# Residual norms by column halves, with a weight subtraction and a cast moved to GpSimd

## The chip, the cores and the metric

One NeuronCore of a Trainium2 chip runs the whole program. The metric is device time in microseconds of that core; each kernel is executed several times and the median stands for it. TensorE is the matrix engine; VectorE (DVE in the profile), ScalarE (ACT) and GpSimd (POOL) do elementwise work; SyncE (SP) issues the DMA transfers. PSUM is the memory of eight banks of 512 fp32 columns that TensorE writes into.

## The reference

The program computes four transformer layers on 256 tokens of width 1024, in fp32: an RWKV-7 layer and an MLA layer with a convolutional gated feed-forward (2816 hidden features) each, then two layers with other attentions and a squared-ReLU MLP. The change is about the first two:

```python
def rmsnorm(x, g):
    xf = x.astype(jnp.float32)
    y = xf * lax.rsqrt(jnp.mean(xf * xf, axis=-1, keepdims=True) + NORM_EPS)
    return (y * g.astype(jnp.float32)).astype(x.dtype)
...
        x = x + rmsnorm(m, norm_g[layer, 1])
        f = conv_ffn(rmsnorm(x, norm_g[layer, 2]), ffn_w_in[layer], ffn_conv_w[layer],
                     ffn_conv_b[layer], ffn_w_out[layer])
        x = x + rmsnorm(f, norm_g[layer, 3])
```

Here m is the output of the layer's mixer behind its output projection, and the norm of a product stands ahead of each addition to x.

## The kernel before, in words

**Data.** The 256 tokens are two tiles (t = 0, 1) of 128 partitions; `x` and `xn` hold 2 x 1024 columns. A product of width 1024 for tile t stands in PSUM banks 2t (columns 0 to 511) and 2t + 1 (columns 512 to 1023). fp32 accuracy comes from splitting each operand into a rounded part (`Ah`, `Bh`, `hTh`, `hidh`) and the rest (`Al`, `Bl`, `hTl`, `hidl`), and adding three products. The rounded weights are made by ScalarE (`round_slot` L1775, `round_a` L1785, `round_b` L1794), the rests by VectorE (`rest_slot` L2514, `rest_a` L2521, `rest_b` L2528) and, for a few slots, by GpSimd (`rest_slot`, L2303).

**Order.** Each engine runs its own program in order; semaphores tie them together. Nothing is planned at run time: the order of each queue is written out by hand.

**Output projection** (`out_proj`, `split_slot`, L877): the first weight slot fills banks 0 and 2, the second banks 1 and 3. The products of tile 0 and then of tile 1 each raise `m_rdy`. Behind it TensorE runs filler products on constants (`keep`, L837) and then `turn16`, which transposes x for the next matmuls. In front of the feed-forward layers this is a product with a diagonal matrix that holds the reciprocal root of the norm (`xn_rdy`, L802), tile by tile; behind them it is a plain transposition that waits for x alone (L800).

**Sites 1 and 3: the norm behind the output projection.** ScalarE (`res_root`, L1745, L1746) squares 1024 columns with a sum and takes the root; VectorE (`res_norm`, L2449, L2450, L2454) takes the reciprocal, scales by it and by the gain row, and adds to x. ScalarE (`norm`, L1699, L1700) squares the new x and takes the root, and VectorE (L2423, L2424) builds the diagonal. On ScalarE `ffn_start(.., 0)`, the cast of the first feed-forward weights, stands ahead of `res_root`, and on VectorE its subtraction stands ahead of `res_norm`.

**The feed-forward** (`ffn`) walks over 11 chunks of 256 hidden features in two halves. `first` (L963 to L971) makes the hidden features, `second` (L991) multiplies them by the second weights into banks 0 to 3, six products per tile and half. The last chunk ends with `second(ch, 0)` and `second(.., 1, last_one=True)`: all of tile 0, then all of tile 1.

**Sites 2 and 4: the norm behind the feed-forward.** VectorE (`res_late`, L2462) multiplies 1024 columns by the gain, ScalarE (`res_root`, L1742) squares the raw product in PSUM behind it and takes the root, and VectorE (L2466, L2468) adds the scaled product to x. Of one PSUM bank, only one of the two engines reads at a time. Behind site 2 ScalarE casts the query weights (`round_m(1)`, L2023, `qdh`), then casts the turned x for the MLA layer (`h2h`, L2084), takes its norm (`late_norm`, L1707, L1714) and casts `hTh` (L2091); VectorE makes the rests (L2917, L3025, L2506) and the latent norm (L2992, L2998), for which TensorE waits (L1339).

Of the kernel before, what the change touches and what calls it, by code (L numbers as in the profile page):

```python
# [84 lines left out]
def program(nc, d, out_d):  # L85
# [4 lines left out]
    with ctx:  # L90
# [30 lines left out]
        gt = sb("gt", [P, 4 * 64])  # L121

# [34 lines left out]
        class Carve:  # L157
# [4 lines left out]
            def __call__(self, n):  # L162
# [16 lines left out]
        a_used = sem("a_used")  # L179
        ah_rdy = sem("ah_rdy")  # L180
# [69 lines left out]
              ["hi", "lo",  # L250
# [527 lines left out]
        def _(pe):  # L778
# [5 lines left out]
            def turn16(name):  # L784
# [143 lines left out]
            def ffn(w, nf):  # L928
# [47 lines left out]

                def second(ch, half, first_one=False, last_one=False):
# [30 lines left out]
                def step(ch, par):  # L1008
# [5 lines left out]
                    second(ch, 0)  # L1014

                chunk_walk(pe, w, step)
                second(NCH[w] - 1, 1, last_one=True)
# [325 lines left out]
            def down(i, b0, w, hi, lo, hi_rdy, lo_rdy):  # L1343
# [4 lines left out]
                pe.wait_ge(dn["hi"], i + 1)  # L1348
# [126 lines left out]
            pe.wait_ge(dn["hi"], 4)  # L1475
# [7 lines left out]
            for s in range(2):  # L1483
                pe.wait_ge(dn["hi"], 5 + s)
# [177 lines left out]
        def _(act):  # L1662
# [74 lines left out]
            def res_root(mi):  # L1737
                for t in range(NT):
                    m = ps[:, 2 * t:2 * t + 2, :].rearrange("p b n -> p (b n)")
                    if mi in MG:  # L1740
                        act.wait_ge(mg_rdy, 2 * MG[mi] + t + 1)
                        link(A_(m, m, ACT.Square, accum_out=st[:, 8 + t:9 + t]))  # L1742
                    else:
                        act.wait_ge(m_rdy, 2 * mi + t + 1)
                        link(A_(xn[:, t, :], m, ACT.Square, accum_out=st[:, 8 + t:9 + t]))  # L1745
                    A_(st[:, 10 + t:11 + t], st[:, 8 + t:9 + t], ACT.Sqrt, bias=eps, scale=1.0 / D  # L1746
                       ).then_inc(msd_rdy, 1)
# [279 lines left out]
            res_root(1)  # L2027
            round_m(1, a_loaded[a_qd], 32 * (a_at["qd"] // 2 + 1))
# [120 lines left out]
            for half in range(2):  # L2149
                round_slot(a_at["wo1"] + 1, half)  # L2150
            ffn_start("ffn1", 0)
            res_root(2)
            norm("nf1")
# [4 lines left out]
            res_root(3)  # L2158
# [108 lines left out]
        def _(pool):  # L2267
# [29 lines left out]

            def rest_slot(a, half):
# [101 lines left out]
        def _(dve):  # L2400
# [43 lines left out]
            def res_norm(mi, gain, following):  # L2444

                dve.wait_ge(rows_in, 16)
                for t in range(NT):
                    dve.wait_ge(msd_rdy, 2 * mi + t + 1)
                    link(V.reciprocal(st[:, 12 + t:13 + t], st[:, 10 + t:11 + t]))  # L2449
                    link(V.scalar_tensor_tensor(xn[:, t, :], mview(t), st[:, 12 + t:13 + t], row(gain),  # L2450
                                                ALU.mult, ALU.mult))
                    if t == 1:
                        norm(following, [0])
                    V.tensor_tensor(x[:, t, :], x[:, t, :], xn[:, t, :], ALU.add).then_inc(x_done, 2)  # L2454
                dve.wait_ge(x_done, x_at(mi, 1))

            def res_late(mi, gain):

                dve.wait_ge(rows_in, 16)
                for t in range(NT):  # L2460
                    dve.wait_ge(m_rdy, 2 * mi + t + 1)
                    V.tensor_tensor(xn[:, t, :], mview(t), row(gain), ALU.mult).then_inc(mg_rdy, 1)  # L2462
                dve.wait_ge(mg_rdy, 2 * MG[mi] + 2)
                for t in range(NT):
                    dve.wait_ge(msd_rdy, 2 * mi + t + 1)
                    link(V.reciprocal(st[:, 12 + t:13 + t], st[:, 10 + t:11 + t]))  # L2466
                    for o0, o1 in ((0, D),) if t == 0 else ((0, 512), (512, D)):
                        V.scalar_tensor_tensor(x[:, t, o0:o1], xn[:, t, o0:o1], st[:, 12 + t:13 + t],  # L2468
                                               x[:, t, o0:o1], ALU.mult, ALU.add
                                               ).then_inc(x_done, (o1 - o0) // 512)  # L2470
                dve.wait_ge(x_done, x_at(mi, 1))

            def res_plain(mi, name=None):
                if name:
                    late_scale(name)
                for t in range(NT):
                    if t == 0 or not name:
                        dve.wait_ge(m_rdy, 2 * mi + t + 1)
                    for o0, o1 in ((0, D),) if t == 0 else ((0, 512), (512, D)):
                        if t and name:  # L2480
                            if o0:
                                dve.wait_ge(m_rdy, 2 * mi + 2)
                            else:
                                dve.wait_ge(half_rdy, {"nm0": 1, "nm1": 2}[name])
# [422 lines left out]
            ffn_start("ffn0", 0)  # L2907
            res_norm(0, "g0_res", "nf0")
            norm("nf0", [1])
            turned_split("nf0", "g0_ffn")  # L2910
            ffn_start("ffn0", 1)
            ffn("ffn0", 0)

            def rest_m(i):

                dve.wait_ge(dn["hi"], i + 1)
# [453 lines left out]
```

## Time and profile before

| | us |
|---|---|
| median of 3 runs | 1356.43 |
| lowest and highest | 1354.27, 1356.81 |
| the profiled execution | 1354.54 |
| its span, first to last instruction | 1352.8 |
| TensorE busy | 1318.0 (97%) |
| VectorE busy | 934.7 (69%) |
| ScalarE busy | 654.6 (48%) |
| GpSimd busy | 96.2 (7%) |

Busy times are sums over the whole span; an engine that is not the last to finish in a stage may stand still at no cost. The chain that ended last is followed back from the last instruction, at each step to what released it. Times within the span count from its first instruction.

### The profile page before, as it was taken

Reading aid. Unit: us, or ns where it says so; the run is one execution under the profiler, and the core shown is the slowest. Engines: PE = TensorE matmul, PEld = TensorE weight load, DVE = VectorE, ACT = ScalarE, POOL = GpSimd, SP = SyncE. Lnnn points to the kernel's source line nnn. Section 1 sums busy time; section 2 is a strip of 40 time slices with the busy share of each in tenths; the row PEclk is TensorE's granted clock in tenths of the full one; section 3 lists DMA queues with packets and bytes.
Section 4 is the critical chain, followed back from the end, with each engine's and each line's share of the span. In section 5 each row is a group of like instructions: output and inputs, shape, how many; then the busy total and the mean of one; then the engine's idle time right before and its main releaser. Section 6 shows DMA issues by size and latency. Waiting matters only on the chain.

```text
span 1352.8 us, 23308 instructions
## 1 busy us (share of the span) xinstructions
PE 1318.0 (97%) x9276; PEld 1134.2 (84%) x9276; DVE 934.7 (69%) x1613; ACT 654.6 (48%) x977; POOL 96.2 (7%) x97
## 2 busy tenths in 40 slices
PE   7999999999999999999999998999999999999999
PEld 5987987888888988888888887888888888888887
DVE  6783356877777775877777588666666796576664
ACT  4431323644445775644444577543334568444441
POOL 0003153000000020000001000000001042000000
PEclk9999999999999999999999999999999999999999
DMA  8531213655553233665551550874531432573610
GB/s 241 215 125 64 66 65 99 226 190 192 192 163 110 70 125 112 219 196 189 186 186 62 187 187 1 311 296 171 202 125 63 165 113 75 205 285 138 243 62 32
DMA packets 111126, 208.10 MB, mean 154 GB/s; under 512 B 3872, under 2 KB 53408, under 8 KB 110528
## 3 DMA queue, kind: packets, MB, share of 16 engines
q1 hardware_dynamic: 111040, 206.88, 44.6%
q8 instruction: 62, 1.02, 0.3%
q14 instruction: 24, 0.20, 0.0%
HBM read 205.82 MB, written 1.05 MB: 153 GB/s over the span
## 4 chain that ended last, share of the span: by engine, by line
PE 85%; DVE 8%; ACT 5%; issue 1%; POOL 0%; DMA 0%; SPq 0%; DVEq 0%; ACTq 0%; POOLq 0%
PE ps L991 21%; PE ps L966 18%; PE ps L877 11%; PE ps L971 10%; PE ps L1060 2%; PE ps L1029 2%; PE ps L1377 2%; PE ps L1163 2%; PE ps L1284 1%; PE ps L942 1%; DVE Al L2514 1%; ACT Ah L1775 1%; PE ps L1420 1%; PE ps L1434 1%; ACT arena L2060 1%
## 5 line engine op out<-in xcount | busy, mean ns | idle before, releaser
L966 PE MATMUL ps<-hTx,Ah 128*128 128x512 f32 x1088 | 270.7, 391 | 0.0
L2521 DVE TENSOR_TENSOR Al<-ringA,Ah 128x2048 fp32r<-128x2048 f32 x76 | 173.8, 2287 | 103.4 <-ACT Ah L1785 103.4
L966 PEld LDWEIGHTS ps<-hTx,Ah 128*128 128x128 f32 x1088 | 199.8, 188 | 38.4
L971 PEld LDWEIGHTS ps<-hTx,Al 128*128 128x128 f32 x1152 | 156.7, 191 | 10.6
L971 PE MATMUL ps<-hTx,Al 128*128 128x256 f32 x1152 | 160.7, 283 | 0.0
L1820 ACT COPY xn<-ps 128x512 f32<-128x512 f32 x72 | 42.3, 587 | 243.6 <-PE ps L971 236.3
L1785 ACT CAST Ah<-ringA 128x2048 fp32r<-128x2048 f32 x76 | 145.8, 1919 | 16.7 <-PE ps L877 13.9
L1794 ACT CAST Bh<-ringB 128x1024 fp32r<-128x1024 f32 (+1 forms) x76 | 107.1, 1409 | 89.5 <-PE ps L991 89.5
L877 PE MATMUL ps<-Ah,hTx 128*128 128x512 f32 (+1 forms) x576 | 136.2, 387 | 1.1 <-ACT hTx L1765 0.9
L991 PE MATMUL ps<-Bh,hidh 128*128 128x512 f32 x432 | 135.0, 392 | 1.6 <-issue 1.1
L991 PE MATMUL ps<-Bl,hidh 128*128 128x512 f32 x432 | 134.3, 390 | 0.0
L2528 DVE TENSOR_TENSOR Bl<-ringB,Bh 128x1024 fp32r<-128x1024 f32 (+1 forms) x76 | 126.9, 1670 | 10.5 <-ACT Bh L1794 10.0
L991 PE MATMUL ps<-Bh,hidl 128*128 128x512 f32 x432 | 134.0, 390 | 0.0
L877 PEld LDWEIGHTS ps<-Ah,hTx 128*128 128x128 f32 x576 | 106.3, 188 | 23.2 <-issue 2.5
L2514 DVE TENSOR_TENSOR Al<-ringA,Ah 128x2048 fp32r<-128x2048 f32 x30 | 68.6, 2289 | 42.4 <-ACT Ah L1775 42.3
L991 PEld LDWEIGHTS ps<-Bl,hidh 128*128 128x128 f32 x432 | 81.1, 188 | 17.6
L991 PEld LDWEIGHTS ps<-Bh,hidl 128*128 128x128 f32 x432 | 81.2, 188 | 17.4
L1775 ACT CAST Ah<-ringA 128x2048 fp32r<-128x2048 f32 (+1 forms) x38 | 71.4, 1878 | 38.5 <-PE ps L877 35.0
L991 PEld LDWEIGHTS ps<-Bh,hidh 128*128 128x128 f32 x432 | 76.4, 189 | 13.8 <-issue 2.3
L2548 DVE TENSOR_TENSOR xn<-ps,xn 128x512 f32<-128x512 f32 x68 | 46.8, 688 | 51.9 <-ACT xn L1820 51.9
L877 PE MATMUL ps<-Al,hTx 128*128 128x512 f32 (+1 forms) x288 | 70.8, 386 | 0.3 <-POOL Al L2303 0.3
L877 PEld LDWEIGHTS ps<-Al,hTx 128*128 128x128 f32 x288 | 53.5, 188 | 11.3 <-POOL Al L2303 0.7
(433 smaller groups left out, 2013.4 us busy)
## 6 DMA issues: line engine op xcount, KB each, us to landing
ringA<-in_ffn_w_in SPq DMA_DIRECT2D x44, 1024.0 KB, 7.5
ringA<-in_mlp_w SPq DMA_DIRECT2D x32, 1024.0 KB, 7.5
ringB<-in_mlp_w SPq DMA_DIRECT2D x32, 1024.0 KB, 6.9
ringB<-in_ffn_w_out SPq DMA_DIRECT2D x44, 512.0 KB, 4.3
ringA<-in_diff_w_in SPq DMA_DIRECT2D x12, 1024.0 KB, 6.3
ringA<-in_dsa_w_in SPq DMA_DIRECT2D x8, 1024.0 KB, 6.4
ringA<-in_w_k SPq DMA_DIRECT2D x4, 1024.0 KB, 8.3
ringA<-in_w_r SPq DMA_DIRECT2D x4, 1024.0 KB, 7.2
```

The lines of the kernel that those rows point to most:

```text
L877: ins = mm(ps[:, banks[t], 0:n], left[:, k, t * P:(t + 1) * P], right[:, half, (k % 4) * n:(k % 4) * n + n], start=(start and k == 0), sto ...
L966: mm(o.rearrange("p (i t) -> p i t", i=2), w_hi, hTx[:, :, k * T:(k + 1) * T], start=(k == 0), stop=False)
L971: last = mm(o[:, T:2 * T], Al[:, half, k * T + j * P:k * T + j * P + P], hTh[:, k, :], start=False, stop=(k == KT - 1))
L991: last = mm(ps[:, 2 * t + c_, :], hb[:, half, f * T + t * P:f * T + t * P + P], wb[:, half, o:o + 512], start=(first_one and f == 0 and i ...
L1775: nc.scalar.copy(k_half(Ah[:, half, :], a, 0), k_half(ringA[:, a % 2, :], a, half)).then_inc(ah_rdy, 1)
L1785: nc.scalar.copy(a_split(w, Ah, half), a_half(w, ap, half)).then_inc(ah_rdy, 1)
L1794: nc.scalar.copy(Bh[:, half, 0:n], ringB[:, bp, half * n:(half + 1) * n]).then_inc(bh_rdy, 1)
L1820: nc.scalar.copy(gup if gelu else hsum, ps[:, b:b + 2, c0:c0 + T]).then_inc(lo_rdy, 1)
L2514: V.tensor_tensor(k_half(Al[:, half, :], a, 0), k_half(ringA[:, a % 2, :], a, half), k_half(Ah[:, half, :], a, 0).bitcast(F32), ALU.subtra ...
L2521: V.tensor_tensor(a_split(w, Al, half), a_half(w, (a_at[w] + par) % 2, half), a_split(w, Ah, half).bitcast(F32), ALU.subtract).then_inc(al ...
L2528: V.tensor_tensor(Bl[:, half, 0:n], ringB[:, (G0[w] + par) % 2, half * n:(half + 1) * n], Bh[:, half, 0:n].bitcast(F32), ALU.subtract).the ...
L2548: V.tensor_tensor(out, ps[:, b:b + 2, T:2 * T], out, ALU.add).then_inc(hs_rdy, 1)
```

## The change

It works on column halves, which are also PSUM banks.

1. In `res_norm` (sites 1 and 3) VectorE multiplies the product by the gain first, half by half; those of columns 0 to 511 of both tiles are done while the second weight slot is still being multiplied. ScalarE squares each half by itself, turns the sum of the first half into a part mean (sum / 1024 + eps, an Identity operation on one column) and takes the root of the second half's sum / 1024 plus that. VectorE then does x + xn * factor in one operation per half. The sums of the new x are formed likewise.
2. The same for `res_late` (sites 2 and 4), in another order, with ScalarE squaring the second bank first into another bank.
3. The last 24 products of the gated feed-forwards are reordered in `second_pair`: tile 0 is whole after 15 products, the first bank of tile 1 after 18.
4. The subtraction of `ffn_start(.., 0)` goes from VectorE to GpSimd (`rest_first`); on ScalarE the first halves' squares stand ahead of its cast.
5. The cast of the query weights goes from ScalarE, ahead of `h2h`, to GpSimd (`dn["hq"]`).
6. Of the two filler products between the turns at sites 1 and 3 one remains.

```diff
@@ PE, turn16
-                                    keep(2, 0)
+                                    keep(1, 0)
@@ PE
+                def second_pair(ch):
+
+                    parts = ((hidh, Bh), (hidh, Bl), (hidl, Bh))
+
+                    def product(half, t, c_):
+                        for i in range(3):
+                            hb, wb = parts[i]
+                            ins = mm(ps[:, 2 * t + c_, :], hb[:, half, t * P:t * P + P],
+                                     wb[:, half, c_ * 512:c_ * 512 + 512],
+                                     start=False, stop=(half == 1 and i == 2))
+                        return ins
+
+                    pe.wait_ge(bl_rdy, ch * 2 + (2 * g0 + 1))
+                    pe.wait_ge(h_rdy, ch * 2 + (2 * g0 + 1))
+                    product(0, 0, 0)
+                    product(0, 0, 1)
+                    product(0, 1, 0)
+                    pe.wait_ge(bl_rdy, ch * 2 + (2 * g0 + 2))
+                    pe.wait_ge(h_rdy, ch * 2 + (2 * g0 + 2))
+                    product(1, 0, 0)
+                    product(1, 0, 1).then_inc(m_rdy, 1)
+                    product(1, 1, 0).then_inc(half_rdy, 1)
+                    product(0, 1, 1).then_inc(b_used, 1)
+                    product(1, 1, 1).then_inc(m_rdy, 1)
...
-                    second(ch, 0)
+                    if nf == 1 and isinstance(ch, int) and ch == NCH[w] - 1:
+                        second_pair(ch)
+                    else:
+                        second(ch, 0)
@@ ScalarE
-            def res_root(mi):
...
+            def square(dst, src, at, ready=None):
+
+                ins = A_(dst, src, ACT.Square, accum_out=hs[:, at:at + 1])
+                if ready is None:
+                    link(ins)
+                else:
+                    ins.then_inc(sq_rdy, 1)
+                    act.wait_ge(sq_rdy, ready)
+
+            def part_mean(dst, at):
+
+                link(A_(hs[:, dst:dst + 1], hs[:, at:at + 1], ACT.Identity, bias=eps, scale=1.0 / D))
+
+            def whole_root(dst, at, part):
+
+                return A_(st[:, dst:dst + 1], hs[:, at:at + 1], ACT.Sqrt, bias=hs[:, part:part + 1],
+                          scale=1.0 / D)
+
+            def res_late_root(mi):
+
+                for t, first, out in ((0, 1, 4), (1, 3, 0)):
+                    act.wait_ge(m_rdy, 2 * mi + t + 1)
+                    square(ps[:, out, :], ps[:, first, :], 4 * t, ready=2 * mi + t + 1)
+                    part_mean(4 * t + 1, 4 * t)
+                    act.wait_ge(wm_rdy, 2 * mi + t + 1)
+                    square(ps[:, first - 1, :], ps[:, first - 1, :], 4 * t + 2)
+                    whole_root(10 + t, 4 * t + 2, 4 * t + 1).then_inc(msd_rdy, 1)
+
+            def first_halves(mi):
+
+                for t in range(NT):
+                    act.wait_ge(wm_rdy, 2 * mi + t + 1)
+                    square(ps[:, 2 * t, :], ps[:, 2 * t, :], 4 * t)
+                    part_mean(4 * t + 1, 4 * t)
+
+            def res_norm(mi):
+
+                def own(t):
+                    act.wait_ge(m_rdy, 2 * mi + t + 1)
+                    square(ps[:, 2 * t, :], ps[:, 2 * t + 1, :], 4 * t + 2, ready=2 * mi + t + 1)
+                    whole_root(10 + t, 4 * t + 2, 4 * t + 1).then_inc(msd_rdy, 1)
+
+                def summed(t, half):
+                    o = slice(512 * half, 512 * half + 512)
+                    act.wait_ge(x_done, x_at(mi, t, half))
+                    square(xn[:, t, o], x[:, t, o], 8 + 4 * t + 2 * half)
+                    if half:
+                        whole_root(2 + t, 10 + 4 * t, 9 + 4 * t).then_inc(rms_rdy, 1)
+                    else:
+                        part_mean(9 + 4 * t, 8 + 4 * t)
+
+                own(0)
+                summed(0, 0)
+                own(1)
+                summed(0, 1)
+                summed(1, 0)
+                summed(1, 1)
@@ ScalarE's order, layer 0 (layer 1 likewise, without the query weights)
+            first_halves(0)
             ffn_start("ffn0", 0)
-            res_root(0)
-            norm("nf0")
+            res_norm(0)
...
-            res_root(1)
-            round_m(1, a_loaded[a_qd], 32 * (a_at["qd"] // 2 + 1))
+            res_late_root(1)
@@ GpSimd
+            def rest_first(w):
+
+                pool.wait_ge(al_rdy, S0[w])
+                pool.wait_ge(ah_rdy, S0[w] + 1)
+                G.tensor_tensor(a_split(w, Al, 0), a_half(w, a_at[w] % 2, 0),
+                                a_split(w, Ah, 0).bitcast(F32), ALU.subtract).then_inc(al_rdy, 1)
...
+            rest_first("ffn0")
+            pool.wait_ge(a_loaded[a_qd], 32 * (a_at["qd"] // 2 + 1))
+            pool.wait_ge(dn["hi"], 1)
+            G.tensor_copy(MW[1][0], MW[1][1]).then_inc(dn["hq"], 1)
             for half in range(2):
                 rest_slot(a_at["wo1"], half)
+            rest_first("ffn1")
@@ VectorE, res_norm
-                for t in range(NT):
-                    dve.wait_ge(msd_rdy, 2 * mi + t + 1)
-                    link(V.reciprocal(st[:, 12 + t:13 + t], st[:, 10 + t:11 + t]))
-                    link(V.scalar_tensor_tensor(xn[:, t, :], mview(t), st[:, 12 + t:13 + t], row(gain),
-                                                ALU.mult, ALU.mult))
-                    if t == 1:
-                        norm(following, [0])
-                    V.tensor_tensor(x[:, t, :], x[:, t, :], xn[:, t, :], ALU.add).then_inc(x_done, 2)
+                dve.wait_ge(*a_free[2 * SPLIT[a_at["wo%d" % (mi // 2)]] + 1])
+                for t in range(NT):
+                    weighted(t, lo).then_inc(wm_rdy, 1)
+                dve.wait_ge(sq_rdy, 2 * mi + 1)
+                link(weighted(0, hi))
+                root(0)
+                summed(0, lo)
+                summed(0, hi)
+                dve.wait_ge(sq_rdy, 2 * mi + 2)
+                link(weighted(1, hi))
+                root(1)
+                summed(1, lo)
+                norm(following, [0])
+                summed(1, hi)
@@ VectorE, res_late
+                dve.wait_ge(m_rdy, 2 * mi + 1)
+                weighted(0, lo).then_inc(wm_rdy, 1)
+                dve.wait_ge(sq_rdy, 2 * mi + 1)
+                weighted(0, hi)
+                dve.wait_ge(half_rdy, mi // 2 + 1)
+                weighted(1, lo).then_inc(wm_rdy, 1)
+                root(0)
+                summed(0, lo)
+                dve.wait_ge(sq_rdy, 2 * mi + 2)
+                link(weighted(1, hi))
+                summed(0, hi)
+                root(1)
+                summed(1, lo)
+                summed(1, hi)
@@ VectorE's order
-            ffn_start("ffn0", 0)
             res_norm(0, "g0_res", "nf0")
             norm("nf0", [1])
             turned_split("nf0", "g0_ffn")
+            dve.wait_ge(al_rdy, S0["ffn0"] + 1)
             ffn_start("ffn0", 1)
```

`weighted(t, o)` is a product of the PSUM columns with the gain row into `xn`, `summed(t, o)` is x + xn * reciprocal root in one operation, and `root(t)` the reciprocal. Waits on `dn["hi"]`, `half_rdy` are renumbered.

## Rows read from the trace of the kernel before

**Rows 1.** The page: TensorE's granted clock by slices, the chain's shares by engine.
```profile
PEclk9999999999999999999999999999999999999999
...
PE 85%; DVE 8%; ACT 5%; issue 1%; POOL 0%; DMA 0%; SPq 0%; DVEq 0%; ACTq 0%; POOLq 0%
```

**Rows 2.** Timeline, site 1: start, length, engine, line, operation, tiles, shapes, count.
```profile
229.63 2.29 DVE L2514 TENSOR_TENSOR Al<-ringA,Ah 128x2048 fp32r<-128x2048 f32 x1 [3.15 <-ACT Ah L1775]
...
233.07 1.91 ACT L1785 CAST Ah<-ringA 128x2048 fp32r<-128x2048 f32 x1 [3.48 <-PE ps L877]
...
235.79 1.03 ACT L1745 ACTIVATE xn<-ps 128x1024 f32<-128x1024 f32 x1 [0.81 <-PE ps L877]
...
236.94 0.29 ACT L1746 ACTIVATE st<-st,con 128x1 f32<-128x1 f32 x1
...
238.32 3.19 PE L837 MATMUL ps<-con 128*128 128x256 f32 x14
...
242.30 2.05 PE L802 MATMUL ps<-arena,x 128*128 128x128 f32 x16 [0.80 <-DVE arena L2424]
...
245.53 2.05 PE L802 MATMUL ps<-arena,x 128*128 128x128 f32 x16 [0.31 <-DVE arena L2424]
```

**Rows 3.** Timeline, site 3: the turn of tile 1.
```profile
548.55 2.05 PE L802 MATMUL ps<-arena,x 128*128 128x128 f32 x16 [0.31 <-DVE arena L2424]
```

**Rows 4.** Timeline, site 2.
```profile
426.67 2.11 ACT L2023 CAST kvdh<-ringA 128x2304 fp32r<-128x2304 f32 x1
...
430.27 2.52 DVE L2462 TENSOR_TENSOR xn<-ps,rows 128x1024 f32<-128x1024 f32 x2 [2.44 <-PE ps L991]
...
434.24 2.77 ACT L2023 CAST qdh<-ringA 128x3072 fp32r<-128x3072 f32 x1
...
434.68 2.18 PE L800 MATMUL ps<-con,x 128*128 128x128 f32 x16 [0.56 <-DVE x L2468]
434.74 1.42 DVE L2468 SCALAR_TENSOR_TENSOR x<-xn,st,x 128x512 f32<-128x512 f32 x2
...
436.90 3.02 ACT L2084 ACTIVATE h2h<-ps,cols 128x256 fp32r<-128x256 f32 x8
```

**Rows 5.** The chain that ended last, behind site 2: start, length, what.
```profile
443.15 3.23 DVE hTx L2506 x8
```

**Rows 6.** Timeline, site 4.
```profile
732.32 0.70 PE L991 MATMUL ps<-Bh,hidh 128*128 128x512 f32 x2 [0.51 <-DVE hidl L2619]
...
738.44 2.18 PE L800 MATMUL ps<-con,x 128*128 128x128 f32 x16 [0.55 <-DVE x L2468]
...
739.79 3.03 ACT L1765 ACTIVATE hTx<-ps,cols 128x256 fp32r<-128x256 f32 x8 [1.70 <-PE ps L800]
```

**Rows 7.** The page's groups: count, busy us, mean ns of one, idle before.
```profile
L1820 ACT COPY xn<-ps 128x512 f32<-128x512 f32 x72 | 42.3, 587 | 243.6 <-PE ps L971 236.3
...
L2548 DVE TENSOR_TENSOR xn<-ps,xn 128x512 f32<-128x512 f32 x68 | 46.8, 688 | 51.9 <-ACT xn L1820 51.9
```

**Rows 8.** GpSimd's subtractions and copy, and VectorE beside them (groups, then timeline).
```profile
L2303 POOL TENSOR_TENSOR Al<-ringA,Ah 128x2048 fp32r<-128x2048 f32 x6 | 27.4, 4564 | 342.7 <-ACT Ah L1775 297.6 <-DVE arena L3239 45.0
...
L2316 POOL COPY rows<-con 128x512 f32<-128x512 f32 x1 | 0.6, 609 | 5.8 <-DMA con<-in_con 5.8
...
1106.90 3.04 POOL L2303 TENSOR_TENSOR Al<-ringA,Ah 128x1312 fp32r<-128x1312 f32 x1 [3.12 <-ACT Ah L1775]
...
1106.96 3.12 DVE L3010 TENSOR_TENSOR arena<-arena 128x128 f32<-128x128 f32 x1
1110.01 0.28 DVE L3011 TENSOR_TENSOR arena<-arena 128x128 f32<-128x128 f32 x1
```

**Rows 9.** Timeline, TensorE's first records.
```profile
4.99 2.93 PE L832 MATMUL ps<-con 128*128 128x128 f32 x12 [4.99 <-DMA con<-in_con]
...
9.80 1.50 PE L832 MATMUL ps<-con 128*128 128x128 f32 x12
```

**Rows 10.** Timeline, ScalarE, between the last Gelu and the first Sqrt of site 2.
```profile
425.26 1.28 ACT L1688 ACT_TABLE_LOAD   x1
```

More of the change, by code:

```diff
@@ L121, in program @@
         gt = sb("gt", [P, 4 * 64])
+        hs = sb("hs", [P, 16])
         Ah = over("Ah", "arena", 0, [P, 2, 2048])
@@ L179, in program @@
         a_used = sem("a_used")
+        wm_rdy, sq_rdy = sem("wm_rdy"), sem("sq_rdy")
         ah_rdy = sem("ah_rdy")
@@ L249, in program @@
         dn = {n: sem("dn_" + n) for n in
-              ["hi", "lo",
+              ["hi", "hq", "lo",
                "h2", "l2",
@@ L1013, in step @@
                     first(ch, 1, single=isinstance(ch, int) and ch == NCH[w] - 1)
-                    second(ch, 0)
+                    if nf == 1 and isinstance(ch, int) and ch == NCH[w] - 1:
+                        second_pair(ch)
+                    else:
+                        second(ch, 0)
                 chunk_walk(pe, w, step)
-                second(NCH[w] - 1, 1, last_one=True)
+                if nf == 2:
+                    second(NCH[w] - 1, 1, last_one=True)
             def feature_job(a0, j0, s, xi):
@@ L2150, in _ @@
                 round_slot(a_at["wo1"] + 1, half)
+            first_halves(2)
             ffn_start("ffn1", 0)
-            res_root(2)
-            norm("nf1")
+            res_norm(2)
             turned_split("nf1", "g1_ffn")
@@ L2157, in _ @@
             prime(ACT.Sqrt)
-            res_root(3)
+            res_late_root(3)
             turned_split("n2", "n0_mix")
@@ L2444, in res_norm, with weighted, root, summed @@
             def res_norm(mi, gain, following):
-                dve.wait_ge(rows_in, 16)
-                for t in range(NT):
+                lo, hi = slice(0, 512), slice(512, D)
+                def weighted(t, o):
+                    return V.tensor_tensor(xn[:, t, o], mview(t)[:, o], row(gain)[:, o], ALU.mult)
+                def root(t):
                     dve.wait_ge(msd_rdy, 2 * mi + t + 1)
                     link(V.reciprocal(st[:, 12 + t:13 + t], st[:, 10 + t:11 + t]))
-                    link(V.scalar_tensor_tensor(xn[:, t, :], mview(t), st[:, 12 + t:13 + t], row(gain),
-                                                ALU.mult, ALU.mult))
-                    if t == 1:
-                        norm(following, [0])
-                    V.tensor_tensor(x[:, t, :], x[:, t, :], xn[:, t, :], ALU.add).then_inc(x_done, 2)
+                def summed(t, o):
+                    V.scalar_tensor_tensor(x[:, t, o], xn[:, t, o], st[:, 12 + t:13 + t], x[:, t, o],
+                                           ALU.mult, ALU.add).then_inc(x_done, 1)
@@ L2455, in res_norm @@
+                summed(1, lo)
+                norm(following, [0])
+                summed(1, hi)
                 dve.wait_ge(x_done, x_at(mi, 1))
             def res_late(mi, gain):
[L2459 to L2464, printed above, removed]
+                lo, hi = slice(0, 512), slice(512, D)
@@ L2465, in res_late, with weighted, root, summed @@
+                def weighted(t, o):
+                    return V.tensor_tensor(xn[:, t, o], mview(t)[:, o], row(gain)[:, o], ALU.mult)
+                def root(t):
                     dve.wait_ge(msd_rdy, 2 * mi + t + 1)
                     link(V.reciprocal(st[:, 12 + t:13 + t], st[:, 10 + t:11 + t]))
[L2467 to L2470, printed above, removed]
+                def summed(t, o):
+                    V.scalar_tensor_tensor(x[:, t, o], xn[:, t, o], st[:, 12 + t:13 + t], x[:, t, o],
+                                           ALU.mult, ALU.add).then_inc(x_done, 1)
@@ L2914, in rest_m @@
             def rest_m(i):
-                dve.wait_ge(dn["hi"], i + 1)
+                dve.wait_ge(*((dn["hi"], 1), (dn["hq"], 1), *((dn["hi"], j) for j in (2, 3, 4, 5)))[i])
                 V.tensor_tensor(MW[i][2], MW[i][1], MW[i][0].bitcast(F32), ALU.subtract
@@ L3086, in _ @@
             turned_split("nf1", "g1_ffn")
+            dve.wait_ge(al_rdy, S0["ffn1"] + 1)
             ffn_start("ffn1", 1)
```

19 lines of the change are left out of this document (6 added, 13 removed).

## The prediction

> **What bounds the kernel now.** I read the page first. TensorE carries 85% of the chain that ended last [rows 1], so nearly everything else is hidden, and a change off TensorE can pay only where TensorE stands still. The change touches four such places, the residual norms behind the two output projections (sites 1 and 3) and behind the two gated feed-forward layers (sites 2 and 4). I then read the timeline of each. At site 1 the projection gives way to filler at 238.32, which lasts until 241.51, and the turn of tile 1 starts only at 245.53 [rows 2]. Between them lies a strict alternation: ScalarE squares 1024 columns, VectorE scales, adds, ScalarE squares the new x, roots, VectorE builds the diagonal. Site 3 is the same to a few hundredths, 303.02 us later [rows 3]. At site 2 what ends last is not the norm: the turns of tile 1 can be read from about 436.0, but ScalarE is in the cast of `qdh` (2.77 us) and starts `h2h` at 436.90; the chain of waits then runs through `h2h` to `hTl` [rows 4, 5]. Site 4 is a norm followed by turns at 738.44 [rows 6].
>
> **Prices.** ScalarE's square of 1024 PSUM columns holds the chain 1.15 us (235.79 to 236.94) [rows 2]; I take the same from SBUF, with 0.03 more. A ScalarE copy of 512 columns lasts 0.587 against 1.03 for 1024, 0.44 less [rows 2, 7]; so I take 0.72 and 0.75 for a square of 512. One-column roots take 0.30 [rows 2]; Identity on one column is not in the trace, and the root is its nearest row: 0.30. VectorE from PSUM, 512 columns: 0.69 [rows 7]; the in-place sum in SBUF, 512: 0.71, half of 1.42 [rows 4].
>
> **Sites 1 and 3, queue by queue.** VectorE ends the last `rest_slot` at 231.92 [rows 2], weights the two first halves until 233.3 (hidden). ScalarE squares them and forms the part means: 2 x (0.72 + 0.30) = 2.05, from 232.65 to 234.7. But behind them in its queue stands the cast for the feed-forward, which before ran at 233.07; it now ends at 236.65 (1.91), and `own(0)`, whose data are ready at 235.79, starts 0.88 late. Then: square 0.72, weighting of the second half 0.69 with the root beside it, reciprocal and its waits 0.25, so the first sum could start at 238.4. With order `own(0), summed(0,0), own(1), ...` the rest is sum 0.71, square 0.75, mean 0.30, square 0.72, weighting 0.69, reciprocal 0.25, sums 0.71, diagonal, sum 0.71, square 0.75, root 0.30, diagonal 0.55: with hand-overs of 0.03 to 0.10 the turn of tile 1 comes at 245.7, against 245.53: +0.2. One filler product is dropped (`keep(1, 0)`), about 0.5 us; it fits a tile-0 turn now at 243.3 instead of 242.30. So without contention the halves give nothing: what is saved on the four squares of 1024 columns (4.7 us) goes to six late ones of 512 (4.4), two means between them (0.6) and the late cast.
>
> The moved subtraction is what decides. On VectorE such a one is 2.29 us, behind the cast and hidden: `res_root` had its data only at 235.79 [rows 2]. On GpSimd it takes about 4.56 us [rows 8], needs the cast, and so runs from 236.7 to 241.2. Its result is needed at 247.3, so by itself it is hidden. But it overlaps the first sum, which reads two SBUF tensors (`xn` and `x`). What that does is in the trace: L3010, 128 columns from two SBUF tensors, lasts 3.12 us from 1106.96, while its twin L3011 right behind takes 0.28; GpSimd's subtraction ran from 1106.90 to 1109.94. So VectorE's instruction was held until about 0.15 us before the end of GpSimd's row. The "GPSIMD Engine Reference" of the Trainium skill (section "Specifications") lists exactly this, contention of the shared SBUF interface with VectorE instructions that have two SBUF inputs; the trace agrees, with 3.12 against 0.28. VectorE reading one PSUM and one SBUF tensor is not held (512-column PSUM rows keep 0.69), so the weightings pass. The first sum is held from 238.4 to 241.05, 2.65 us, and as `own(1)` is queued behind `summed(0,0)`, everything after it slides with it. Site 1: +0.2 + 2.65 = +2.85; with the same at site 3, **+5.7**. Bounds per site: +0.2 if nothing is held, +3.2 if held to the very end of a 4.63 us instruction and the late cast costs a little more.
>
> **Site 2.** `second_pair` reorders 24 products, at 0.23 each the same sum. Tile 0 is whole after 15 products instead of 18: 0.69 earlier, 429.58 instead of 430.27 [rows 4]. From there VectorE: weightings 3 x 0.69, reciprocal 0.2, sum 0.71, weighting 0.69, sum 0.71 = 4.5 us to the end of tile 0, so the turn starts near 434.15 instead of 434.68. The `qdh` cast leaves ScalarE for GpSimd: `h2h` starts when the first pair of banks is turned. At site 4 that is 1.35 after the first turn [rows 6], here 435.5 instead of 436.90: -1.4. VectorE must follow: `rest_m(0)` and `h2l` end at 441.5, just before `hTl` may start at 441.65 instead of 443.15, so the gain passes on down the chain [rows 5]. GpSimd's cast of 3072 columns starts at 428.8, when `kvdh` is cast [rows 4], if the query weights are loaded by then; by its one copy row, 0.609 for 512 [rows 8], it lasts at most 6 x 0.609 = 3.65 and ends by 432.5, 0.5 past the first sum at 431.9; part of that hold is in slack. I take **-1.3**; bounds -1.5, and by GpSimd's two-input rate (4.56/2048 x 3072 = 6.8 us, held until 435.5) +2.3. Its own consumer, `rest_m(1)`, comes at 445, nine microseconds later.
>
> **Site 4.** Here the second half of the hidden features comes late: the products of the second half wait for VectorE's `hidl` until 732.32 [rows 6]. Before, 12 products stood ahead of that wait and 12 behind; now 9 and 15, so the last product ends 0.69 later, while tile 0 (6 products behind the wait) is no earlier. VectorE's 4.5 us from 733.99 give a turn at 738.6 against 738.44: **+0.15**, bounds 0 and +0.9.
>
> Sum: 5.7 - 1.3 + 0.15 = +4.55 us. The profiled execution took 1354.54 (span 1352.8), 1.9 below the median of 1356.43; on the median this gives **1361.0**. About 0.2%, 2.7 us, is what a measurement of this kernel can tell from no change.
>
> **The rivals.**
> *The hold does not occur* (chance 0.20): GpSimd and VectorE might share more finely where the operands lie otherwise. Then +0.4 - 1.3 + 0.15 = -0.75: 1355.7, no change to be told. Against it stands L3010 in rows 8, a single instruction, though ten times its length.
> *The clock falls as well* (0.25). In the hold TensorE stands still from 241.51 to about 246.0, 4.5 us, where before it paused 0.80 there [rows 2]. The only longer pause of the trace is the start, 4.99 us: the twelve records behind it take 2.93 us, the same twelve 1.50 us at 9.80 [rows 9], that is the lower of the two levels, 1.2 GHz, against 2.4; the page's PEclk line stays at 9 in both [rows 1], so durations alone show it. At 4.5 us the pause is nearer to 4.99 than to 0.8, but these are two points only. Price: 1.45 us per site, +4.55 + 1.45 = 1362.5 for one site, 1363.9 for both. The Trainium skill, "TensorE: Matmul & The Clock Gate" (section "Why this matters for your kernels"), says that idle gaps between bursts of matmuls put the clock back; by it this rival would be the forecast.
> *Faster* (0.08). Place: ScalarE's queue at 233 to 236.7. If the first halves come early enough to leave the cast at 233.07 and VectorE isn't held, `own(0)` starts on its data: -0.88 + 0.2 = -0.7 at each of sites 1 and 3, with -1.5 at site 2: -2.9, 1353.5. It needs the first halves done before 233.07; VectorE ends its subtraction only at 231.92, which leaves 1.15 for 2.05 of ScalarE work.
> *GpSimd's cast is slow* (0.03): 1364.6. *Identity needs another table than Sqrt* (0.02): a table load takes 1.28 us [rows 10], two for each of twelve means, 30.7 us, 1387. The Trainium skill, "ScalarE: Activation LUTs" (section "Table sets: the hidden batching unit"), says that identity is in every set; no row here shows it.
>
> **How the numbers follow.** The forecast has 0.42. The range, 1355.6 to 1363.6, reaches from no hold to a clock that falls at one site, and leaves out about 0.2. The forecast's own range is 1359 to 1362.5. Slower by over 0.2%: 0.42, less a tenth for an overestimated hold, plus 0.25 and 0.05, 0.68. Faster: 0.08. Within: the rest, 0.24.
>
> **What would show it.** At sites 1 and 3: GpSimd subtraction from 236.7 for 4.5 us; one sum of 512 columns of about 3.3 us instead of 0.7, ending with it; `own(0)` near 236.7; TensorE idle over 4 us. At site 2: no ScalarE cast between root and `h2h`, `h2h` near 435.5. At site 4: the last product 0.7 later. Wrong would be: sums of 0.7 us under the subtraction, a first half hidden well before 233, or records behind the pause at double length.

## The result, and the profile after

| | before | after |
|---|---|---|
| median of 5 runs, us | 1356.06 (1354.27 to 1356.81) | 1365.11 (1361.8 to 1365.29) |
| profiled execution, us | 1354.54 | 1363.4 |
| its span, us | 1352.8 | 1361.6 |
| its mean granted TensorE clock | 1.000 | 0.995 |

The ratio is 1.0064, with a 95% interval of 1.0053 to 1.0076: the changed kernel is slower by 8.7 us (9.05 between the medians), where +4.6 was forecast. It is slower, as forecast, but the time lies outside the range, whose upper end was 1363.6.

The page of the changed kernel, TensorE's clock by slices and the chain's shares. Before, every slice stood at 9 [rows 1]; now two slices of 34 us, those that hold sites 1 and 3, show 8.

```profile
PEclk9999999899999999899999999999999999999999
...
PE 86%; DVE 6%; ACT 6%; issue 1%; POOL 0%; DMA 0%; SPq 0%; ACTq 0%; DVEq 0%; POOLq 0%
```

The timeline of the changed kernel at site 1 (columns as in [rows 2]; the site comes 0.18 us later than before, by the end of the last projection product).

```profile
234.83 1.91 ACT L1862 CAST Ah<-ringA 128x2048 fp32r<-128x2048 f32 x1
...
236.64 0.58 ACT L1770 ACTIVATE ps<-ps 128x512 f32<-128x512 f32 x1
236.91 4.56 POOL L2378 TENSOR_TENSOR Al<-ringA,Ah 128x2048 fp32r<-128x2048 f32 x1 [20.82 <-ACT Ah L1862]
...
237.38 0.69 DVE L2537 TENSOR_TENSOR xn<-ps,rows 128x512 f32<-128x512 f32 x1 [4.07 <-ACT ps L1770]
...
238.30 4.38 DVE L2544 SCALAR_TENSOR_TENSOR x<-xn,st,x 128x512 f32<-128x512 f32 x2
...
242.05 0.63 ACT L1770 ACTIVATE xn<-x 128x512 f32<-128x512 f32 x1 [4.38 <-DVE x L2544]
...
245.98 3.79 PE L804 MATMUL ps<-arena,x 128*128 128x128 f32 x16 [4.29 <-DVE arena L2512]
...
249.56 1.06 PE L839 MATMUL ps<-con 128*128 128x256 f32 x2
250.41 2.16 PE L804 MATMUL ps<-arena,x 128*128 128x128 f32 x16
252.33 0.49 PE L944 MATMUL ps<-hTx,Ah 128*128 128x256 f32 x2
```

Two things are to be seen. The two sums at 238.30 take 4.38 us. The first of them alone takes 3.72 us, to 242.02, where one that nothing delays takes 0.75; GpSimd's subtraction ends at 241.47, so the sum was held until about 0.2 us before that end. I call this the hold. ScalarE's next square starts at 242.05. The second thing is on TensorE: the turn of tile 0 (its 16 transposing products) at 245.98, behind a pause of 4.29 us, takes 3.79 us where it took 2.05 [rows 2]. The windows show why (length, busy us of PE, PEld, DVE, ACT and POOL with counts, granted clock, DMA share, GB/s):

```profile
242.00:245.00 3.00, 0.00 (x0) 0.00 (x0) 1.76 (x5) 2.82 (x9) 0.00 (x0) 0.84 1.02 411
245.00:248.00 3.00, 2.02 (x9) 2.02 (x10) 1.71 (x5) 2.12 (x7) 0.00 (x0) 0.50 0.16 66
248.00:251.00 3.00, 3.00 (x15) 2.82 (x14) 0.29 (x1) 0.00 (x0) 0.00 (x0) 0.53 0.00 0
```

The granted clock is 0.50 there, the lower of the two levels (1.2 GHz). TensorE stood still until 245.98, and by shorter windows the clock falls near 244.0, in the pause, and comes back only near 250.8; the diagonal of tile 1 is ready at 248.3, but its turn waits for TensorE's own slow work until 250.41. At site 3 the same stretch reads:

```profile
543.23 4.55 POOL L2378 TENSOR_TENSOR Al<-ringA,Ah 128x2048 fp32r<-128x2048 f32 x1 [33.19 <-ACT Ah L1862]
...
544.65 4.34 DVE L2544 SCALAR_TENSOR_TENSOR x<-xn,st,x 128x512 f32<-128x512 f32 x2
...
552.29 3.78 PE L804 MATMUL ps<-arena,x 128*128 128x128 f32 x16 [4.30 <-DVE arena L2512]
...
556.72 2.58 PE L804 MATMUL ps<-arena,x 128*128 128x128 f32 x16
```

Sites 2 and 4 of the changed kernel, which answer to [rows 4, 6]:

```profile
431.70 2.11 ACT L2100 CAST kvdh<-ringA 128x2304 fp32r<-128x2304 f32 x1
...
433.94 2.76 POOL L2470 CAST qdh<-ringA 128x3072 fp32r<-128x3072 f32 x1 [192.47 <-ACT kvdh L2100]
...
436.85 0.75 DVE L2576 SCALAR_TENSOR_TENSOR x<-xn,st,x 128x512 f32<-128x512 f32 x1
...
440.39 3.03 ACT L2160 ACTIVATE h2h<-ps,cols 128x256 fp32r<-128x256 f32 x8 [1.73 <-PE ps L802]
...
740.91 0.47 PE L986 MATMUL ps<-Bh,hidh 128*128 128x512 f32 x1 [1.20 <-DVE hidl L2742]
...
748.41 3.04 ACT L1842 ACTIVATE hTx<-ps,cols 128x256 fp32r<-128x256 f32 x8 [1.73 <-PE ps L802]
```

From ScalarE's cast of `kvdh` to `h2h` it was 10.23 us and is 8.69: 1.54 gained. The gain is passed on: from the cast of `kvdh` to the start of the last projection product of site 3 it was 113.76 us and is 112.19. GpSimd's cast ends at 436.70, before the first sum, which keeps its 0.75 us. At site 4, from the product that waits for `hidl` to ScalarE's cast of the turned x, it was 7.47 and is 7.50.

**The account** (the other kernels are those of the next section). What runs before site 1 is the same in all of them, and yet the last projection product ends anywhere between 238.4 and 241.1 in their profiled executions. In the six where it ends last, at 239.2 or later, TensorE's granted clock is 0.91 in one stretch of 20 us (from 20 to 40 us, in `e2_filler` from 180 to 200), and in the other five it is 1.00 in every such stretch. So I measure each site by itself: from the end of the last projection product to the first feed-forward product (sites 1 and 3), and from `kvdh` to `h2h` (site 2). Each figure comes from the one execution that was profiled. Before, at site 1, that is from 237.41 + 1.08 to 247.34, which is 8.85:

```profile
237.41 1.08 PE L877 MATMUL ps<-Al,hTx 128*128 128x512 f32 x4
...
247.34 0.48 PE L942 MATMUL ps<-hTx,Ah 128*128 128x256 f32 x2
```

| kernel | site 1, us | site 3, us | site 2, us | sum of the three against before, us | ratio measured |
|---|---|---|---|---|---|
| before | 8.85 | 8.85 | 10.23 | | |
| after | 13.66 | 14.09 | 8.69 | +8.5 | 1.0064 [1.0053, 1.0076] |
| `e2_filler` | 11.50 | 11.52 | 8.69 | +3.8 | 1.0032 [1.0020, 1.0044] |
| `e3_sub_dve_cast_first` | 10.54 | 10.54 | 8.69 | +1.8 | 1.0009 [0.9999, 1.0018] |
| `e9_sub_dve_long_filler` | 9.07 | 9.07 | 8.69 | -1.1 | 0.9999 [0.9990, 1.0008] |
| `e8_split8` | 10.64 | 10.70 | 8.69 | +2.1 | 1.0012 [1.0003, 1.0021] |
| `e7_gpsimd_sub_only` | 9.54 | 9.49 | 10.23 | +1.3 | 1.0015 [1.0006, 1.0025] |
| `e10_short_filler` | 10.88 | 9.73 | 10.22 | +2.9 | 1.0026 [1.0014, 1.0038] |
| `e4_gpsimd_cast_only` | 8.85 | 8.85 | 9.36 | -0.9 | 0.9995 [0.9986, 1.0004] |
| `e5_late_no_gpsimd_cast` | 8.85 | 8.85 | 9.62 | -0.6 | 0.9996 [0.9987, 1.0005] |
| `e6_late_only` | 8.85 | 8.86 | 8.80 | -1.4 | 0.9989 [0.9980, 0.9998] |

A ratio of 0.001 is 1.36 us, and each sum lies within its measured interval. The loss sits at sites 1 and 3. The kernel before was timed again beside each group of experiments, with medians of 1355.50, 1355.04 and 1355.78 us, so the ratios are to be compared and not the bare medians.

### The profile page after: what moved, and what is told of

Same layout as the page of the kernel before. It is cut to its first block, busy times and chain, and to the rows that moved or that the text cites. A ratio compares the mean times of both kernels' runs of the same rounds, so it can differ in the third digit from the quotient of the medians.

```text
span 1361.6 us, 23361 instructions
## 1 busy us (share of the span) xinstructions
PE 1321.4 (97%) x9272; PEld 1137.9 (84%) x9272; DVE 937.8 (69%) x1625; ACT 658.8 (48%) x1012; POOL 108.1 (8%) x100
## 3 DMA queue, kind: packets, MB, share of 16 engines
HBM read 205.82 MB, written 1.05 MB: 152 GB/s over the span
## 4 chain that ended last, share of the span: by engine, by line
PE 86%; DVE 6%; ACT 6%; issue 1%; POOL 0%; DMA 0%; SPq 0%; ACTq 0%; DVEq 0%; POOLq 0%
PE ps L1018 21%; PE ps L968 18%; PE ps L879 11%; PE ps L973 10%; PE ps L1091 2%; PE ps L1060 2%; PE ps L1408 2%; PE ps L1194 2%; PE ps L1315 1%; PE ps L944 1%; ACT Ah L1852 1%; PE ps L804 1%; PE ps L1451 1%; PE ps L1465 1%; PE ps L839 1%
## 5 line engine op out<-in xcount | busy, mean ns | idle before, releaser
L2644 DVE TENSOR_TENSOR Al<-ringA,Ah 128x2048 fp32r<-128x2048 f32 x74 | 169.3, 2287 | 97.4 <-ACT Ah L1862 97.4
L1018 PE MATMUL ps<-Bh,hidh 128*128 128x512 f32 x416 | 129.9, 392 | 1.1 <-issue 1.1
L1018 PE MATMUL ps<-Bl,hidh 128*128 128x512 f32 x416 | 129.2, 390 | 0.0
L1018 PE MATMUL ps<-Bh,hidl 128*128 128x512 f32 x416 | 129.0, 390 | 0.0
L2637 DVE TENSOR_TENSOR Al<-ringA,Ah 128x2048 fp32r<-128x2048 f32 x30 | 68.6, 2289 | 42.4 <-ACT Ah L1852 42.2
L1018 PEld LDWEIGHTS ps<-Bl,hidh 128*128 128x128 f32 x416 | 78.1, 188 | 17.0
L1018 PEld LDWEIGHTS ps<-Bh,hidl 128*128 128x128 f32 x416 | 78.1, 188 | 16.7
L1018 PEld LDWEIGHTS ps<-Bh,hidh 128*128 128x128 f32 x416 | 73.6, 189 | 12.5 <-issue 1.4
```

What stands on the lines that cost most here:

```text
L1018: last = mm(ps[:, 2 * t + c_, :], hb[:, half, f * T + t * P:f * T + t * P + P], wb[:, half, o:o + 512], start=(first_one and f == 0 and i ...
L2637: V.tensor_tensor(k_half(Al[:, half, :], a, 0), k_half(ringA[:, a % 2, :], a, half), k_half(Ah[:, half, :], a, 0).bitcast(F32), ALU.subtra ...
L2644: V.tensor_tensor(a_split(w, Al, half), a_half(w, (a_at[w] + par) % 2, half), a_split(w, Ah, half).bitcast(F32), ALU.subtract).then_inc(al ...
```

## The experiments

**Is the lost time hold or clock?** The changed kernel with TensorE kept busy through the hold:

```diff
-            keep(7, 7)
+            keep(16, 7)
             turn16("nf0")
```
and the same for `nf1`.

> The changed kernel, with 16 filler products instead of 7 ahead of the turns at sites 1 and 3, so that TensorE does not stand still while VectorE is held. Nothing else differs. Theory (hold by GpSimd 2.7 us per site, and behind the 4.3 us pause some 2.1 us per site from TensorE at its lower level): the held sum stays at about 3.6 us, the turn of tile 0 takes 2.05 us again instead of 3.79, the turn of tile 1 starts about 2.7 us later than before instead of 4.7; in all about +4 us on before, near 1360. Rival (the slow turns come from the shorter filler between the turns, or from memory traffic, not from the pause): the turn stays near 3.8 us and the time near 1365.

```profile
240.70 4.38 DVE L2544 SCALAR_TENSOR_TENSOR x<-xn,st,x 128x512 f32<-128x512 f32 x2
240.91 7.07 PE L839 MATMUL ps<-con 128*128 128x256 f32 x32
...
248.38 2.05 PE L804 MATMUL ps<-arena,x 128*128 128x128 f32 x16 [0.40 <-DVE arena L2512]
```

1359.61 us. The hold is as long as in the changed kernel, the pause is 0.40 us, and the turns are back at 2.05. The site is 2.65 us longer than in the kernel before, 2.67 at site 3, and that is the hold. It is 2.16 and 2.57 us shorter than in the changed kernel, and that is the clock.

**The clock alone.** The kernel before, with only its filler cut:

```diff
-            keep(7, 7)
+            keep(1, 7)
             turn16("nf0")
```
and the same for `nf1`.

> The kernel before, in which only the filler ahead of the two turns of the feed-forward norms is cut from 14 matmuls to 2, so that TensorE pauses 3.5 us in place of 0.8. The data path is untouched. If the second half of what the changed kernel loses is the price of the clock alone, the granted clock shows a dip at each site, the first turn takes 3.1 to 3.8 us, and the time is 1.5 to 2.1 us longer for each site: 1359 to 1360.3. If the clock needs the hold as well to fall, or its price is only the 1.45 us of the prediction for one site, the time is 1356.1 to 1357.5.

```profile
239.09 0.60 PE L837 MATMUL ps<-con 128*128 128x256 f32 x2
...
243.07 3.78 PE L802 MATMUL ps<-arena,x 128*128 128x128 f32 x16 [3.38 <-DVE arena L2424]
246.65 1.91 PE L837 MATMUL ps<-con 128*128 128x256 f32 x4
248.35 2.03 PE L802 MATMUL ps<-arena,x 128*128 128x128 f32 x16
```

1359.0 us. ScalarE and VectorE run as before; a pause of 3.38 us makes the turn 3.78 and the site 2.03 longer. At site 3 the same pause cost 0.88, less than the 1.5 to 2.1 expected for each site: TensorE was at the lower level for half as long there. Together that is 2.9 of the 3.5 us measured; in this execution TensorE ran slower at site 2 too, where nothing was edited and the pause ahead was the 1.0 us of the kernel before (2.52 us for ten products that take 1.60).

```profile
442.74 2.52 PE L1361 MATMUL ps<-kvdh,h2h 128*128 128x288 f32 x10 [0.19 <-ACT h2h L2084]
```

**Without the hold.** The subtraction is back on VectorE, behind the two first weightings, and ScalarE's cast stands ahead of the first halves:

```diff
@@ ScalarE, VectorE, GpSimd
-            first_halves(0)
             ffn_start("ffn0", 0)
+            first_halves(0)
...
                     weighted(t, lo).then_inc(wm_rdy, 1)
+                ffn_start("ffn%d" % (mi // 2), 0)
...
-            rest_first("ffn0")
```

> The changed kernel, with the subtraction of the first feed-forward weights back on VectorE (behind the weighting of the two first halves), and on ScalarE its cast ahead of the squares of the first halves. Theory: no VectorE operation with two SBUF inputs meets GpSimd, the first sum lasts 0.75 us, the pause of TensorE ahead of the turn of tile 0 is near 2 us and the turn takes 2.05 us; sites 1 and 3 cost +0.3 to +0.5 us each, site 2 keeps its -1.5: about 1355.5. Rival (the halves themselves, with their part means and order, cost the time): the sites stay at +4 us or more each and the time above 1361.

```profile
239.03 1.41 DVE L2542 SCALAR_TENSOR_TENSOR x<-xn,st,x 128x512 f32<-128x512 f32 x2
...
243.74 3.06 PE L804 MATMUL ps<-arena,x 128*128 128x128 f32 x16 [1.85 <-DVE arena L2510]
246.60 1.06 PE L839 MATMUL ps<-con 128*128 128x256 f32 x2
247.45 2.21 PE L804 MATMUL ps<-arena,x 128*128 128x128 f32 x16
```

The granted clock there (columns as in the windows above):

```profile
244.00:244.50 0.50, 0.50 (x6) 0.50 (x6) 0.35 (x1) 0.40 (x3) 0.00 (x0) 1.00 0.96 385
244.50:245.00 0.50, 0.50 (x5) 0.50 (x4) 0.00 (x0) 0.50 (x2) 0.00 (x0) 0.56 1.02 418
```

1356.87 us, 1.4 above what was expected. The sums are not held, but the turn is slow already behind 1.85 us, and the clock falls only near 244.6, when the turn has been running since 243.74. To see whether the pause does it, the same kernel with `keep(11, 7)` for `keep(7, 7)`:

> The kernel of the run with the subtraction on VectorE and ScalarE's cast first, with 22 filler matmuls in place of 14 ahead of the turns, which cover the pause of 1.85 us. If the slower turns of that run (3.06 and 2.56 us in place of 2.05) come from the pause, both turns are back at 2.05 us, and the time falls by 1.0 to 1.4 us at each site: about 1354.3. If they come from something else, the time stays at 1356.9.

```profile
238.79 4.91 PE L839 MATMUL ps<-con 128*128 128x256 f32 x22
243.82 2.05 PE L804 MATMUL ps<-arena,x 128*128 128x128 f32 x16
...
246.22 2.05 PE L804 MATMUL ps<-arena,x 128*128 128x128 f32 x16
```

1355.09 us, 0.8 above what was expected. Both turns are at 2.05, and each site is 1.47 us shorter. It is still 0.22 longer than in the kernel before: in this order the halves at sites 1 and 3 bring nothing even with no hold and a full clock. The medians differ by 1.8 us, the sites by 2.9; both lie within the intervals. The executions of the kernel without the long filler run from 1354.27 to 1357.53 us, with mean granted clocks from 0.999 down to 0.996, so some of them may have lost less to the clock than the profiled one, at 1356.8.

**The subtraction alone.** The kernel before, with the subtraction moved to GpSimd:

```diff
@@ GpSimd, VectorE
+            rest_first("ffn0")
             for half in range(2):
                 rest_slot(a_at["wo1"], half)
+            rest_first("ffn1")
...
-            ffn_start("ffn0", 0)
             res_norm(0, "g0_res", "nf0")
```
and the same for `ffn1`; VectorE waits for `al_rdy` ahead of `ffn_start(.., 1)`.

> The kernel before with the subtraction of ffn0's and ffn1's first slot moved from VectorE to GpSimd and nothing else. GpSimd then runs it from 235.0 to 239.6, and the operations of VectorE that fall in it are the whole weighted sum of tile 0. If a VectorE operation of that kind is held until GpSimd's instruction ends, the sum at 238.9 is held some 0.5 us at each site, TensorE's pause ahead of the turn is about 1.3 us, and the time is 1357 to 1358. If there is no hold unless two operations collide by their start, the time is 1356.0; if the VectorE time saved by the move counts (2.6 us less of it ahead of the norm), below 1355.

```profile
237.19 4.60 POOL L2302 TENSOR_TENSOR Al<-ringA,Ah 128x2048 fp32r<-128x2048 f32 x1 [19.26 <-ACT Ah L1785]
...
239.56 1.28 DVE L2459 SCALAR_TENSOR_TENSOR xn<-ps,st,rows 128x1024 f32<-128x1024 f32 x1
240.95 1.92 DVE L2463 TENSOR_TENSOR x<-x,xn 128x1024 f32<-128x1024 f32 x1
```

1357.37 us. The scaling from PSUM runs wholly beside GpSimd's instruction and keeps its 1.28 us; the add of two SBUF tensors right behind it takes 1.92, where its twin for tile 1 takes 1.22. The sites are 0.69 and 0.64 longer. VectorE's freed 2.3 us are worth nothing.

**One long instruction or eight short ones.** The changed kernel, its subtraction cut into eight of 256 columns:

```diff
-                G.tensor_tensor(a_split(w, Al, 0), a_half(w, a_at[w] % 2, 0),
-                                a_split(w, Ah, 0).bitcast(F32), ALU.subtract).then_inc(al_rdy, 1)
+                for q in range(8):
+                    ins = G.tensor_tensor(a_split(w, Al, 0)[:, q], a_half(w, a_at[w] % 2, 0)[:, q],
+                                          a_split(w, Ah, 0)[:, q].bitcast(F32), ALU.subtract)
```

> The changed kernel, with GpSimd's subtraction at sites 1 and 3 cut into eight instructions of 256 columns, each waiting for the one before. Theory (a VectorE operation with two SBUF inputs is held until the running GpSimd instruction ends, and no longer): the first sum is held 0.7 us at most and the following ones likewise, GpSimd's eight take 5 to 6 us; the turn of tile 1 starts 1 to 1.5 us later than before, the pause is near 3 us; 1356.5 to 1359. Rival (it is held as long as GpSimd has work queued): the first sum lasts 4 us or more, the time is 1365 or more.

```profile
237.95 7.93 POOL L2379 TENSOR_TENSOR Al<-ringA,Ah 128x256 fp32r<-128x256 f32 x8 [20.82 <-ACT Ah L1862]
...
239.33 1.89 DVE L2548 SCALAR_TENSOR_TENSOR x<-xn,st,x 128x512 f32<-128x512 f32 x2
...
242.84 1.12 DVE L2548 SCALAR_TENSOR_TENSOR x<-xn,st,x 128x512 f32<-128x512 f32 x1
...
244.07 0.56 DVE L2516 TENSOR_SCALAR arena<-con,st 128x128 f32<-128x128 f32 x1
```

Two of the eight by themselves, the second and the third:

```profile
238.77 0.74 POOL L2379 TENSOR_TENSOR Al<-ringA,Ah 128x256 fp32r<-128x256 f32 x1
...
239.59 1.08 POOL L2379 TENSOR_TENSOR Al<-ringA,Ah 128x256 fp32r<-128x256 f32 x1
```

1356.6 us. GpSimd takes 7.93 us in place of 4.56, yet the two sums wait only 0.48 us in all, the later one 0.37, and the diagonal, built from SBUF, 0.27. So VectorE waits for the GpSimd instruction that is running, not for its queue. The eight were expected to take 5 to 6 us. Four of them take 0.72 to 0.74 us; the four that start while one of VectorE's sums is running take 1.05 to 1.25, the one at 239.59 until the first sum (239.33 to 240.08) is out of the way. So the two engines hold each other, each until the other's running instruction is nearly over, and by an estimate 1.5 of the 7.93 us are GpSimd's own waits (what the four take beyond 0.74 each). The pause of 1.96 us still brings a slow turn.

**The late norms alone.** Sites 1 and 3 as in the kernel before; `second_pair`, the halves of `res_late` and GpSimd's cast as in the changed one.

```diff
-            first_halves(0)
             ffn_start("ffn0", 0)
-            res_norm(0)
+            res_root(0)
+            norm("nf0")
...
-            rest_first("ffn0")
```

> Sites 1 and 3 as in the kernel before (whole-tile norm, subtraction on VectorE, two filler products between the turns); sites 2 and 4, the reordered last products and GpSimd's cast of the query weights as in the changed kernel. Theory: the whole loss lies at sites 1 and 3 and this part gains 1.5 us at site 2 and nothing at site 4: about 1354.5, ratio 0.9989. Rival (the gain at site 2 is taken back further on, or the reordered products cost at site 4): 1356 or more.

1354.64 us, ratio 0.9989 [0.9980, 0.9998]: the upper end is just below 1, so this version is faster than the kernel before, by about 1.5 us by the ratio (0.9 by the medians), and its ratio is the lowest of all. One interval of ten that just misses 1 is thin by itself; the 1.4 us read from the sites say the same. Its two parts by themselves, first the kernel before with GpSimd's cast alone:

```diff
@@ ScalarE, GpSimd
-            round_m(1, a_loaded[a_qd], 32 * (a_at["qd"] // 2 + 1))
...
+            pool.wait_ge(dn["hi"], 1)
+            G.tensor_copy(MW[1][0], MW[1][1]).then_inc(dn["hq"], 1)
```

> The kernel before with one part of the change: GpSimd rounds qd's matrix in place of ScalarE, all four residual norms as before. If the earlier start of the residual norm behind attention comes mainly from ScalarE being free of this cast, h2h starts about 0.9 us earlier and the time is about 1355.1. If it comes from the halves (weighting and square per bank, one sum, root of two sums), nothing moves: 1356.0. With the one look at the halves alone kept for later, a value between the two divides the gain.

then the late norms without it (ScalarE casts behind `res_late_root(1)`):

```diff
             res_late_root(1)
+            nc.scalar.copy(MW[1][0], MW[1][1]).then_inc(dn["hq"], 1)
```

> The run with the late norms alone changed, but ScalarE still rounds qd's matrix, behind the squares of the residual norm as in the kernel before. The run with GpSimd's cast alone brought h2h 0.87 us nearer to the cast of kvd, the late norms with the cast 1.43 us. If the two parts add, the halves alone bring 0.56 us, and the time is about 1355.5 where the kernel before is at 1356.0. If ScalarE's cast of 2.77 us stands ahead of h2h whatever the norm does, h2h comes no earlier than in the kernel before (10.2 us behind the cast of kvd, within 0.2), the halves alone are worth nothing, and the time is 1356.0.

The `h2h` of the one, then of the other, whose ScalarE goes from the last root straight to the cast:

```profile
437.54 3.03 ACT L2083 ACTIVATE h2h<-ps,cols 128x256 fp32r<-128x256 f32 x8 [1.70 <-PE ps L800]
```
```profile
433.56 2.74 ACT L2084 CAST qdh<-ringA 128x3072 fp32r<-128x3072 f32 x1
436.20 3.02 ACT L2140 ACTIVATE h2h<-ps,cols 128x256 fp32r<-128x256 f32 x8
```

The cast alone brings `h2h` 0.87 us forward and the halves alone 0.61, 1.48 together, and both at once 1.43: they add. The second theory for the halves alone fell. The cast does stand ahead of `h2h`, but the halves end ScalarE's last root earlier, and the cast starts with it. Neither part's ratio (0.9995, 0.9996) can be told from 1 by itself; the traces carry this.

## Why the prediction was right and wrong

**The hold: right**, in mechanism and size. GpSimd runs from 236.91 for 4.56 us (forecast 236.7), the first sum is held until about 0.2 us before its end (forecast 0.15), and the weightings are free. A site with the clock held up is 2.65 us longer (`e2_filler`), against 2.85. The difference is in the queue estimate: `own(0)` started 0.67 late instead of 0.88, and the first sum could have started at 238.30, or 238.12 without the offset, instead of 238.4. The two sums lost 2.97 (4.38 against 1.41). So without a hold the changed order would have made a site some 0.3 us shorter than before, not 0.2 longer. That is worked out; no kernel ran that order without the hold.

**The clock: the step that failed.** The forecast's sum left out the term that the rival "the clock falls as well" priced at 1.45 us a site, and gave that rival 0.25 because the pause of 4.5 us lay between only two points, 0.80 and 4.99. The pause came as forecast, 4.29, and the clock fell at both sites, at 2.16 and 2.57 us each. Two errors lie in this. The pause was part of the forecast already, and the nearer row was the slow one [rows 9]; the term belonged in the sum. And the price was taken from twelve records alone, 2.93 against 1.50 (1.43, taken as 1.45): here a turn of 16, the filler and part of the next turn ran at the lower level. The range then took in a clock that falls at one site of two, though the sites are copies of each other. With 2.65 and 2.37 per site in place of 2.85 and 0, the sum is 5.3 + 4.7 - 1.5 = +8.5. The Trainium skill, "TensorE: Matmul & The Clock Gate" (section "Why this matters for your kernels"), had the rule that idle gaps between bursts put the clock back; `e10_short_filler` shows it with no other edit; here pauses of 1.85 us were already enough at two sites (`e3_sub_dve_cast_first`).

**Site 2: right**, 1.54 gained against 1.3. GpSimd's cast took 2.76 us, below the bound of 3.65, and ended before the first sum, where an end 0.5 behind it was allowed for; the bound of +2.3 was far off.

**Site 4: right.** The last product ends 0.70 later behind its wait (740.91 + 3.67 against 732.32 + 2.97), and VectorE's halves take it back: +0.03 against +0.15.

**The other rivals.** "No hold" and "GpSimd's cast is slow" fell by these rows. "Faster" fell by its own condition: the first halves ran at 232.74 and the cast at 234.83, not 233.07. Identity and Sqrt shared a table: the part mean at 233.46 takes 0.29 and no load stands beside it.

## What to carry to other kernels

Work moved to GpSimd is not free for VectorE even where its result is needed late. Look in its span for VectorE operations that work on SBUF tensors alone, and price the one that comes next as held nearly to the end of the running GpSimd instruction. A longer stall of TensorE can carry a second price, the turns behind it at half rate. Count it in the sum once the pause is longer than those the trace shows at full speed, at every copy of the site; filler that covers the pause takes it off. And take a change apart: here the part at sites 2 and 4 gained 1.5 us and the part at sites 1 and 3 lost 10.

## What the runs showed of the hardware

- VectorE's sums of two SBUF tensors and its diagonal of 128 columns from SBUF were held beside GpSimd's subtraction. Its products of a PSUM and an SBUF tensor (0.69 us for 512 columns, 1.28 for 1024) and its one-column reciprocal (0.16 at 238.10 in the changed kernel) were not. GpSimd's subtractions were held in turn by sums already running (1.05 to 1.25 us against 0.72 to 0.74, `e8_split8`).
- The clock doesn't go by the pause alone. Turns kept 2.05 us behind 0.80 and 1.49 us (`e7_gpsimd_sub_only`); behind 1.85 they took 3.06 at site 1 and 2.56 at site 3, and the site lost 1.47 both times; behind 3.38 they took 3.78 and 3.51, and the sites lost 2.03 and 0.88; behind 4.29, 2.16 and 2.57. One stretch fell with no pause longer than before (`e10_short_filler`, site 2). Six of the eleven profiled executions lose clock ahead of site 1 too (0.91 over 20 us), where all the kernels are the same. And one and the same pause of 3.38 us left TensorE at the lower level for 6.8 us at site 1 of `e10_short_filler` (241.7 to 248.5) and for 3.4 us at site 3 (548.9 to 552.3), which is why its price differs. What else decides stays open.
- GpSimd casts 128 x 3072 from fp32 in 2.76 us, as fast as ScalarE (2.77 [rows 4]), while its subtraction of 128 x 2048 takes 4.56, twice VectorE's 2.29 [rows 2].
- A GpSimd subtraction cut in eight takes 1.7 times as long beside VectorE's sums (7.93 against 4.56; by an estimate 6.4 without its own waits, 7.93 less 1.5), and VectorE's waits fall from 2.97 to 1.12 us (0.48 + 0.37 + 0.27).
